# Four k groups in both halves of a feed-forward output, and later vector work in the feed-forward input

## The reference, cut to what matters

```
h = rms_norm(x, ffn_pre_gain)                      # 256 x 2048
gt, up = split(h @ w_ffn_in)                       # two halves of 256 x 5632
x = x + rms_norm((silu(gt) * up) @ w_ffn_out, ffn_post_gain)
```

## Time and profile before

| | |
|---|---|
| median of 3 runs | 1489.25 us (1489.09 to 1489.53) |
| the profiled execution's own time | 1489.06 us |
| its span | 1487.2 us |
| TensorE matmuls busy | 1476.5 us (99%) |
| VectorE busy | 1142.4 us (77%) |
| ScalarE busy | 863.1 us (58%) |
| GpSimd busy | 151.5 us (10%) |

### The profile page before, as it was taken

The page is one execution under the profiler, slowest core; times in us unless marked ns, Lnnn a source line. Parts: engine busy times, 40 slices in busy tenths (PEclk is TensorE's granted clock), DMA queues, the critical chain, the costliest instruction groups (busy, mean ns, idle before and its releaser), DMA issues.

```text
span 1487.2 us, 19430 instructions
## 1 busy us (share of the span) xinstructions
PE 1476.5 (99%) x6676; PEld 1212.7 (82%) x6676; DVE 1142.4 (77%) x1338; ACT 863.1 (58%) x1054; POOL 151.5 (10%) x286
## 2 busy tenths in 40 slices
PE   9999999999999999999999999999999999999997
PEld 7888887888888888888888888888888888888886
DVE  6878988855554587657476879999999876897897
ACT  6645455565666544656668556666666654554653
POOL 0000000050220000000000112221122221200000
PEclk9999999999999999999999999999999999999999
DMA  9755555565565655866555574555666667556555
GB/s 340 239 189 175 182 176 191 188 209 186 186 195 172 235 185 178 332 199 214 170 178 190 178 264 165 203 196 219 234 226 214 210 191 246 185 187 223 174 182 196
DMA packets 89859, 305.08 MB, mean 205 GB/s; under 512 B 13056, under 2 KB 13568, under 8 KB 88768
## 3 DMA queue, kind: packets, MB, share of 16 engines
q1 hardware_dynamic: 80144, 285.12, 57.0%
q0 software_dynamic: 9216, 18.63, 3.8%
q10 hardware_dynamic: 432, 0.45, 0.1%
HBM read 294.19 MB, written 2.10 MB: 199 GB/s over the span
## 4 chain that ended last, share of the span: by engine, by line
PE 95%; DVE 3%; issue 1%; ACT 1%; DVEq 0%; POOL 0%; ACTq 0%; POOLq 0%
PE acc L1897 10%; PE acc L1899 10%; PE acc L1898 10%; PE side L2202 5%; PE side L2204 5%; PE side L2203 5%; PE side L1897 3%; PE side L1899 3%; PE side L1898 3%; PE tr L1899 3%; PE tr L1897 3%; PE tr L1898 3%; PE acc L2202 3%; PE acc L2204 3%; PE acc L2203 3%; PE side L2190 2%
## 5 line engine op out<-in xcount | busy, mean ns | idle before, releaser
L634 ACT ACTIVATE w_hi<-raw 128x1024 fp32r<-128x1024 f32 x321 | 338.8, 1060 | 259.6 <-PE side L2204 103.0
L1123 DVE TENSOR_TENSOR w_lo<-raw,w_hi 128x1024 fp32r<-128x1024 f32 x262 | 320.7, 1227 | 201.8 <-ACT w_hi L616 197.4
L1128 DVE TENSOR_TENSOR w_lo<-raw,w_hi 128x1024 fp32r<-128x1024 f32 x333 | 399.0, 1219 | 93.5 <-ACT w_hi L634 83.9
L616 ACT ACTIVATE w_hi<-raw 128x1024 fp32r<-128x1024 f32 x262 | 276.9, 1059 | 280.7 <-PE acc L1899 164.8
L1897 PE MATMUL acc<-w_hi,xT_hi 128*128 128x512 f32 x504 | 198.3, 393 | 0.0
L1899 PE MATMUL acc<-w_hi,xT_lo 128*128 128x512 f32 x504 | 196.3, 389 | 0.0
L1898 PE MATMUL acc<-w_lo,xT_hi 128*128 128x512 f32 x504 | 196.3, 389 | 0.0
L589 POOL DMA_DIRECT2D hT_st<-h_blk x176 | 93.6, 540 | 499.1 <-DVE h_blk L1175 471.0
L1897 PEld LDWEIGHTS acc<-w_hi,xT_hi 128*128 128x128 f32 x504 | 94.6, 188 | 21.9 <-issue 2.0
L1899 PEld LDWEIGHTS acc<-w_hi,xT_lo 128*128 128x128 f32 x504 | 94.6, 188 | 20.0
L1898 PEld LDWEIGHTS acc<-w_lo,xT_hi 128*128 128x128 f32 x504 | 94.7, 188 | 19.1
(11 more groups left out here) (482 smaller groups left out, 2880.0 us busy)
## 6 DMA issues: line engine op xcount, KB each, us to landing
raw<-in_units SPq DMA_DIRECT2D x530, 512.0 KB, 4.2
hT_st<-h_blk POOLq DMA_DIRECT2D x176, 32.0 KB, 2.7
x_tok<-in_x SPq DMA_DIRECT2D x4, 512.0 KB, 5.8
qkT<-qk_blk POOLq DMA_DIRECT2D x64, 32.0 KB, 3.1
xres<-in_x POOLq DMA_DIRECT2D x1, 2048.0 KB, 11.1
m_raw<-in_mem_t POOLq DMA_DIRECT2D x1, 2048.0 KB, 8.8
mq<-in_mem POOLq DMA_DIRECT2D x1, 2048.0 KB, 15.6
x_raw<-in_x_t SPq DMA_DIRECT2D x6, 256.0 KB, 6.1
```

Source lines behind the costliest of these rows:

```text
L616: a_.activation(w_hi[:, j % RING], raw[:, j % RING], ACT.Copy).then_inc(hi_ready, 1)
L634: a_.activation(w_hi[:, v % RING], late_raw[slot], ACT.Copy).then_inc(hi_ready, 1)
L1123: v_.tensor_tensor(w_lo[:, s], raw[:, s], w_hi[:, s].bitcast(F32), ALU.subtract).then_inc(lo_ready, 1)
L1128: v_.tensor_tensor(lo[:, v % RING], late_raw[slot], hi[:, v % RING].bitcast(F32), ALU.subtract).then_inc(lo_ready, 1)
```

## The change

It has five parts.

1. Half 0 of the output gets a fourth k group (28 products and 28 plain units, before 21 and 32), and starts with 8 plain units in place of 6. Half 1 takes its groups in the order 3, 1, 2, 0, so that the sums of group 3 serve both halves; those of group 0 are made again for the end of half 1 (`SUMS`).
2. The block difference for P7 moves from `max(at P5 + 1, v - 2)` to `max(at P5 - 1, v - 3)`, in the input and in the output.
3. In the input, `hidden_product` and `hidden_lo` move one step later.
4. Around the start of the output, the sums of group 1 are made early, `hidden_hi(10)` and `hidden_lo(10)` move from steps 2 and 4 to 8 and 10, and `hidden_turn(11)` moves from 6 to 2.
5. `hidden_hi(11)` moves from step 16 to 25 and `hidden_lo(11)` from 20 to 28 (the steps are counted from the first unit of the output, `S_FO`, as 0).

```diff
-OUT_GROUPS = ((0, 1, 2), (0, 1, 2, 3))
-SUMS = (0, 1, 2, 3)
-SUMS_OF = ((1, 2), (3,))
+OUT_GROUPS = ((0, 1, 2, 3), (3, 1, 2, 0))
+SUMS = (0, 1, 2, 3, 0)
+SUMS_OF = ((2, 3), (4,))
@@ out_segment
-    return spread(plain, products, len(plain) - 4 - 4 * m, 6 - 2 * m)
+    return spread(plain, products, len(plain) - 4 - 4 * m, 8 - 4 * m)
@@ late_units
             if kind == "P7":
-                wanted.append((max(at["P5", g] + 1, v - 2), b12, b22, b12, 0, v))
+                wanted.append((max(at["P5", g] - 1, v - 3), b12, b22, b12, 0, v))
@@ buffers
-        h_f = [... (164, 48, 48, 60, 60) ...]
-        H_f = [... (120, 52, 52, 52, 52) ...]
+        h_f = [... (164, 160, 48, 48, 60) ...]
+        H_f = [... (120, 116, 52, 52, 52) ...]
@@ scalar, sums_hi
                 if k == 2:
                     act.wait_ge(hT_ready, 11)
                 if k == 3:
-                    act.wait_ge(unit_used, OUTS[1].first + OUTS[1].order.index(("P4", 0)) + 1)
+                    act.wait_ge(unit_used, OUTS[0].first + OUTS[0].order.index(("P4", 0)) + 1)
+                if k == 4:
+                    act.wait_ge(unit_used, OUTS[1].first + OUTS[1].order.index(("P4", 3)) + 1)
@@ scalar, output
                     if v == S_FO + 1:
                         sums_hi(0)
-                    if v == S_FO + 2:
+                    if v == S_FO + 4:
+                        sums_hi(1)
+                    if v == S_FO + 8:
+                        act.wait_ge(hs_lo, 2)
                         hidden_hi(10)
-                    if v == S_FO + 16:
+                    if v == S_FO + 25:
                         hidden_hi(11)
@@ vector, input
-                    if i > 1 and v == b.first:
+                    if i > 1 and v == b.first + (i > 2):
                         hidden_product(i - 2)
-                    if i > 2 and v == b.first + 3:
+                    if i > 2 and v == b.first + 4:
                         hidden_lo(i - 2)
@@ vector, before the output
                     hidden_sums(0)
+                if v == BODIES[9].end + 9:
+                    hidden_sums(1)
@@ vector, output
                     if m == 1 and v == b.first + 10:
-                        hidden_sums(3)
+                        hidden_sums(4)
-                    if v == S_FO + 3:
+                    if v == S_FO + 2:
+                        dve.wait_ge(hT_turned, 10 * 256)
+                        hidden_turn(11)
+                    if v == S_FO + 4:
                         hidden_sums_lo(0)
-                    if v == S_FO + 4:
+                    if v == S_FO + 6:
+                        hidden_sums_lo(1)
+                    if v == S_FO + 10:
                         hidden_lo(10)
-                    if v == S_FO + 6:
-                        hidden_turn(11)
-                    if v == S_FO + 20:
+                    if v == S_FO + 28:
                         hidden_lo(11)
@@ tensor, P5
-                        pe.wait_ge(hs_lo, g + 1)
+                        pe.wait_ge(hs_lo, 5 if (m, g) == (1, 0) else g + 1)
```

More of the change, by code:

```diff
@@ L341, in trunk @@
         e_sb = at("e_sb", 200, [NC])
-        h_f = [at(f"h_f{k}", kb, [4, SEQ]) for k, kb in enumerate((164, 48, 48, 60, 60)[:len(SUMS)])]
-        H_f = [at(f"H_f{k}", kb, [4, 2, P]) for k, kb in enumerate((120, 52, 52, 52, 52)[:len(SUMS)])]
+        h_f = [at(f"h_f{k}", kb, [4, SEQ]) for k, kb in enumerate((164, 160, 48, 48, 60)[:len(SUMS)])]
+        H_f = [at(f"H_f{k}", kb, [4, 2, P]) for k, kb in enumerate((120, 116, 52, 52, 52)[:len(SUMS)])]
         H_hi = [at(f"H_hi{k}", kb, [4, 2, P], F32R) for k, kb in enumerate((72, 168, 176))]
```

## The result

The changed kernel takes 1496.76 us (median of 5 runs, 1496.26 to 1497.65) and the kernel before 1489.53 us beside it. The ratio is 1.0049 (95% interval 1.0037 to 1.006), so it is slower by 7.2 us. The forecast was 1496.0, with 1490.8 to 1498.5 as the range. The profiled execution has a span of 1495.0 us, 7.8 more than before.

The account below looks back on a forecast made before the run. TensorE's matmuls (busy 99%) were taken as the bound, if VectorE (77%) keeps up. -1.4 + 3.0 + 4.6 + 0.7 = +6.9 us on 1489.06 gave 1496.0 us, range 1490.8 to 1498.5.

Parts of the forecast that it names:

- six matmuls fewer: Output half 0: four plain units (48 matmuls) become seven products (42), at 0.227 us per matmul: -1.4 us.
- input, bodies 3 to 8: Input: gate7's stall goes, P2 waits 1.05 us plus 0.11, each body loses 0.5 us more: +3.0 us.
- output half 0: Half 0: late last-chunk rounding and VectorE's list give four stalls (2.5, 0.65, 0.35, 0.65), 0.11 each: +4.6 us.
- output half 1: Half 1: a group 1 n0 stalls 0.35 and 0.11, the last group's P7 comes 0.29 later: together +0.7 us.
- the 0.29 us wait: VectorE: a difference right behind the w_lo it waits for starts after 1.43 us, 0.29 more than 1.14.
- the second place: Half 0, unit 34 after unit 32's stall: its w_lo usable at 20.95 against 20.30, a stall of 0.65 us.
- the two of group 3: Half 0, group 3: units 43 and 45 wait for their w_lo, stalls of 0.35 and 0.65 us.
- At nothing: Moves at output steps 0 to 10, hidden_turn(11)'s DMA wait, loads and the tail were forecast to cost nothing.
- A: Rival: all cover holds, half 0's idle VectorE hides everything and input stalls go: -5.0, 1484.1 us; chance 0.08.
- B: Rival: the input gains, the output loses; P7's difference costs P2 nothing: +0.3, 1489.4 us; chance 0.06.
- C: Rival: output stalls are covered, sums_hi finds hidden_lo(11) done, input as forecast: +2.3, 1491.4 us; chance 0.09.
- D: Rival: loads come late too, one wait in each half adds 2 to 4 us: 1499 us; chance 0.07.

Follow-up runs that it names:

- e1: Kernel before with only the input's part of the change (P7's difference earlier, hidden_product and hidden_lo one step later, bodies 3 to 8): 1492.59 us, ratio 1.0020.
- e3: Changed kernel with only P7's difference put back to its old place in the input: 1495.77 us, 1.0 less than the changed kernel.
- e10: Kernel before with only P7's difference one or two steps earlier, in the input and both output halves: 1491.41 us, ratio 1.0012.
- e7: Changed kernel with only hidden_lo put back to step 3 in the input: 1495.06 us, 1.7 less than the changed kernel.
- e4: Kernel before with hidden_lo moved from step 3 to 1 and hidden_turn from 6 to 10 in bodies 3 to 10: 1488.37 us, ratio 0.9993.
- e5: As e4, but hidden_turn is late only in bodies 3 to 8: 1485.96 us, ratio 0.9978 to the kernel before.
- e6: Changed kernel with hidden_hi(11) at step 20 in place of 25 and hidden_lo(11) at 22 in place of 28: 1494.58 us.
- e9: e8 with half 0's products spread over one more plain unit and sums, rounding, low part 8, 5, 4 steps ahead of P5: 1484.95 us, ratio 0.9969.
- e8: Four groups in both halves, e5's input, P7's difference as before, e6's rounding, half 0's sums, rounding, low part 10, 7, 6 steps ahead of P5: 1487.56 us.
- e2: Changed kernel with the input as before, the output keeping all of the change: 1494.10 us, ratio 1.0031 to the kernel before.

## Why the prediction was right, point by point

The sum was +6.9 us; the runs say +7.2. The steps, by the start times of the two profiled executions:

| step | predicted | measured |
|---|---|---|
| six matmuls fewer | -1.4 | -1.4 (6676 to 6670) |
| input, bodies 3 to 8 | +3.0 | +3.1 (0.52 per body; alone in e1 +3.0) |
| output half 0 | +4.6 | +4.9 (losses 2.64, 0.68, 0.24, 0.52, 0.65) |
| output half 1 | +0.7 | +0.5 |
| sum | +6.9 | +7.1 of the span's +7.8 |

- *Input.* The place (P2), the reason (the difference for P7 and the 0.29 us wait in front of its `w_lo`) and the size (1.05 + 0.11 against 1.11 + 0.08) are right. The 0.5 us per body are 0.52. e3 and e10 show both parts of it apart, e7 the 0.29 us wait, and e4 and e5 that the length of the list is what counts.
- *Half 0.* Unit 32 was forecast 2.5 us late and lost 2.57; the second place 0.65 and 0.57, the two of group 3 0.35 and 0.65 for 0.45 and 0.54. Missed was unit 40, with 0.16 + 0.08: I had not worked out that n1. The five sums of group 3 stand in front of its `w_lo`. e6 takes away the one wait and leaves the others. Part of the near match of the sum is luck: the missed 0.24 us are made up for by the 0.2 us too much in half 1.
- *Half 1.* 0.35 + 0.11 forecast, 0.44 + 0.07 measured at unit 73. The last group's P7 lost 0.06 and 0.10 where it had lost 0.10 before, not 0.3 more. The 0.29 us wait is there (a difference at 1449.23, with 0.20 idle). But P7's own difference has moved ahead of the sums' low part, so that from the low part to P7's `w_lo` are 3.70 us (1446.67 to 1450.37), before 4.76 (1437.83 to 1442.59). I had added the wait and not taken the difference off.
- *"At nothing".* The moves at steps 0 to 10 of the output left no wait there, and the wait of `hidden_turn(11)` for DMAs delays nobody. Loads were not late: from 1180 us on, five roundings waited for a DMA, 2.2 us at most, where it had been nine and 4.4 us. In the first part of the span, which the change doesn't touch, the trace has one wait of 0.8 us (L1907 for `w_lo`) that the trace of before lacks, and the first product starts 0.63 us later. Ten of the eleven traces of the experiments have 0.2 to 0.6 us at the same place (L1897 or L1907, at 13 us), and in all eleven the first product starts 0.1 to 0.7 us later than in the trace of before. So that is no part of the change, and it makes up what is between 7.1 and 7.8.

The rivals: A would need VectorE's idle time to be where the work is. It is not: e9 shows that 9.7 us more of VectorE work (103.6 in place of 93.9 us in the stretch of half 0) fit without a wait over 0.2 us, but only with other places. B and C fall with e1 and the 2.4 us wait. D did not happen.

The place where I was wrong is in the experiments: e4 missed the two short bodies, e8's places were worse than my lists said they would be, and the 3.4 us that e1 and e2 were to show were counted from losses and not from start times.

## What to carry to other kernels

When an engine is filled over a stretch, write down its instructions from the first point at which it is idle to the unit that waits, and add them up. Moving one within that list changes which unit waits and how long (1.3 to 1.8 us over six bodies in e3, e7 and e10), and some unit still waits; moving it out of the list takes the waits away (e5: 3.4 us with no instruction removed). Two instructions on different engines that depend on each other must not be put at the same step of a shared order: the step is where each engine is free to do it, and the queue behind the waiting one pays (2.6 us here). Put an unrelated instruction between one and the one that waits for it on the same engine.

## What the runs showed of the hardware

- A VectorE instruction that waits by semaphore for the one right in front of it starts 1.42 us after it, and 1.14 us after it where it doesn't wait or another stands between (e7). The cost is in the time, 1.7 us for six bodies. The Trainium skill ("VectorE: DVE Perf Modes", section "The DRAIN you can't avoid") says from eight `tensor_copy` that the semaphore costs nothing extra; for 128x1024 float32 `tensor_tensor` these runs disagree.
- After a wait of TensorE the first matmul is 0.08 to 0.11 us longer than the others (0.47 to 0.50 us in place of 0.39), and the second starts that much later. The same is seen where the `w_lo` comes just in time and no wait is listed (gate7 in e5: 0.50 us at 948.85, its `w_lo` started 1.27 us before).
- In e3 the granted clock was 0.51 from 1320.00 to 1323.30 us, behind a wait of 2.40 us in which TensorE did nothing; its matmuls came 0.43 us apart. In three other traces the clock stayed at 1.00 behind a wait as long.
- The 16 small DMAs that spread a turned chunk take 13.7 us from the first issue to the point where ScalarE can use the result (e4). Their issue on GpSimd is 8.5 us of it.
